# Gated recurrence of a two-block mixer: transposes before state products, the next head's preparation on other levels, masks and values loaded first

## What is computed

```python
def chunk_scan(q, k, v, logf, s0):
    """S_t = diag(f_t) S_{t-1} + k_t v_t^T, o_t = S_t^T q_t, chunkwise. q,k,logf (B,L,H,K); v (B,L,H,V)"""
    def step(S, inp):
        qb, kb, vb, gb = inp
        G = jnp.cumsum(gb, axis=1)
        o_inter = jnp.einsum('bthk,bhkv->bthv', qb * jnp.exp(G), S)
        decay = jnp.exp(jnp.where(earlier_or_same, G[:, :, None] - G[:, None, :], -jnp.inf))
        A = jnp.einsum('bthk,bshk,btshk->bhts', qb, kb, decay)
        o_intra = jnp.einsum('bhts,bshv->bthv', A, vb)
        S_new = jnp.exp(G[:, -1])[..., None] * S + jnp.einsum('bshk,bshv->bhkv', kb * jnp.exp(G[:, -1:] - G), vb)
        return S_new, o_inter + o_intra
```

## Time and profile before

| | us |
|---|---|
| median of three runs | 3906.14 |
| profiled execution | 3909.69 |
| its span | 3907.7 |
| TensorE busy | 3560.9 (91%) |
| VectorE busy | 2585.6 (66%) |
| ScalarE busy | 1877.3 (48%) |
| GpSimd busy | 790.5 (20%) |

### The profile page before, as it was taken

One profiled execution on the slowest core, in us unless ns is written; L12 is line 12 of the kernel. 1 busy time (PEld: TensorE's weight loads), 2 busy tenths in 40 slices (PEclk: granted clock), 3 DMA queues, 4 the chain that ended last, 5 costly groups with the idle time before them and its releaser, 6 DMA issues. The chain is left out here.

```text
span 3907.7 us, 43104 instructions
## 1 busy us (share of the span) xinstructions
PE 3560.9 (91%) x16760; PEld 2846.0 (73%) x16760; DVE 2585.6 (66%) x2881; ACT 1877.3 (48%) x2428; POOL 790.5 (20%) x624
## 2 busy tenths in 40 slices
PE   7999889964697999999999998999898989999989
PEld 4887744664685888888878786788776678787857
DVE  6546266876767888889888887556575545516753
ACT  5211111355463777767777776342464323515731
POOL 2100025500021110111111114210243223203422
PEclk9999989977897999999999999999998999999999
DMA  5554314220236999999999996365411433525133
GB/s 198 201 186 143 124 43 172 84 110 19 94 139 228 379 366 382 378 366 379 376 372 370 362 379 200 107 208 178 168 54 56 164 109 110 165 103 186 48 102 119
DMA packets 322788, 774.50 MB, mean 198 GB/s; under 512 B 26072, under 2 KB 110419, under 8 KB 322328
## 3 DMA queue, kind: packets, MB, share of 16 engines
q1 hardware_dynamic: 299802, 694.94, 48.9%
q0 software_dynamic: 17856, 66.33, 5.2%
q10 hardware_dynamic: 4928, 10.49, 0.8%
HBM read 660.21 MB, written 111.48 MB: 197 GB/s over the span
## 5 line engine op out<-in xcount | busy, mean ns | idle before, releaser
L3398 DVE TENSOR_TENSOR first_expert_w_low<-shared_z,first_expert_w_high 128x2048 fp32r<-128x2048 f32 x127 | 297.1, 2380 | 80.0 <-ACT first_expert_w_high L3351 79.5
L3398 DVE TENSOR_TENSOR moe_w_low<-moe_w_raw,moe_w_high 128x2048 fp32r<-128x2048 f32 x128 | 287.3, 2285 | 52.6 <-ACT moe_w_high L3351 52.1
L3398 DVE TENSOR_TENSOR moe_w_low<-shared_z,moe_w_high 128x2048 fp32r<-128x2048 f32 x128 | 290.5, 2310 | 19.9 <-ACT moe_w_high L3351 19.9
L3351 ACT ACTIVATE first_expert_w_high<-shared_z 128x2048 fp32r<-128x2048 f32 x126 | 234.9, 1918 | 121.0 <-DMA shared_z<-in_exp_w 118.4
L3351 ACT ACTIVATE moe_w_high<-moe_w_raw 128x2048 fp32r<-128x2048 f32 x128 | 238.3, 1911 | 91.2 <-DMA moe_w_raw<-in_exp_w 83.9
L3626 POOL TENSOR_SCALAR layer_att_p<-layer_att_p,layer_att_rinv,layer_att_neg_lam 128x1280 f32<-128x1280 f32 (+1 forms) x72 | 173.4, 2408 | 529.9 <-DVE layer_att_neg_lam L3655 314.2
L3351 ACT ACTIVATE moe_w_high<-shared_z 128x2048 fp32r<-128x2048 f32 x128 | 238.5, 1915 | 54.1 <-DMA shared_z<-in_exp_w 48.3
L177 PE MATMUL moe_bank<-moe_w_high,first_expert_xgT_high 128*128 128x512 f32 x640 | 252.7, 395 | 0.0
L3633 DVE TENSOR_REDUCE layer_att_nb<-layer_att_scores 128x1 f32<-128x1280 f32 (+1 forms) x144 | 195.0, 1369 | 86.4 <-PE layer_att_scores L3538 85.4
L178 PE MATMUL moe_bank<-moe_w_low,first_expert_xgT_high 128*128 128x512 f32 x640 | 250.8, 392 | 0.0
L179 PE MATMUL moe_bank<-moe_w_high,first_expert_xgT_low 128*128 128x512 f32 x640 | 250.6, 391 | 0.0
(11 more groups left out here) (660 smaller groups left out, 9522.1 us busy)
## 6 DMA issues: line engine op xcount, KB each, us to landing
shared_z<-in_exp_w SPq DMA_DIRECT2D x128, 2048.0 KB, 10.1
moe_w_raw<-in_exp_w SPq DMA_DIRECT2D x64, 2048.0 KB, 9.9
shared_z<-in_w_in SPq DMA_DIRECT2D x48, 512.0 KB, 6.2
first_raw<-in_w_in SPq DMA_DIRECT2D x32, 512.0 KB, 7.3
front_vec<-in_ada_w POOLq DMA_DIRECT2D x16, 1024.0 KB, 6.0
proj_t<-front_out SPq DMA_DIRECT2D x48, 256.0 KB, 2.0
shared_z<-in_w_mod SPq DMA_DIRECT2D x24, 512.0 KB, 4.5
k_high<-layer_front_staged SPq DMA_DIRECT2D x20, 512.0 KB
```

The lines of the kernel that those rows point to most:

```text
L3351: nc.scalar.activation(hi, x, ACT.Copy).then_inc(high, 1)
L3398: nc.vector.tensor_tensor(lo, x, hi.bitcast(F32), ALU.subtract).then_inc(low, 1)
```

## The change

Three edits, no instruction added or taken away. SP issues the masks and the values ahead of q and z of head 1. ScalarE does the next head's preparation on other levels: queries at level 1 instead of 5, sigmoids at 2 and 4 instead of 2 and 3, gates at 3 and 5 instead of 3 and 4. TensorE transposes the keys of a level ahead of the state products instead of behind them.

```diff
@@ -2317,10 +2317,10 @@
+                sp.dma_start(mask[:, :, :], io["t_pair_masks"][:, 0:LEVELS * P].rearrange("p (i t) -> p i t", t=P)).then_inc(masks, 16)
+                sp.dma_start(v[:, :, :], core.vg[:, 0:BANK].rearrange("(t p) c -> p t c", p=P)).then_inc(inputs, 16)
                 load_q(1)
                 load_z(1)
-                sp.dma_start(mask[:, :, :], io["t_pair_masks"][:, 0:LEVELS * P].rearrange("p (i t) -> p i t", t=P)).then_inc(masks, 16)
-                sp.dma_start(v[:, :, :], core.vg[:, 0:BANK].rearrange("(t p) c -> p t c", p=P)).then_inc(inputs, 16)
                 for h in range(1, H):
@@ -2427,13 +2427,13 @@
                         if h >= 2 and j in (1, 2):
                             o_copy(2 * (h - 2) + j - 1)
-                        if more and j in (3, 4):
-                            gates(h + 1, j - 3)
-                        if more and j in (2, 3):
+                        if more and j in (3, 5):
+                            gates(h + 1, j // 2 - 1)
+                        if more and j in (2, 4):
                             if (h, j) == (0, 2):
                                 act.wait_ge(zeroed, 1)
-                            sigmoids(h + 1, j - 2)
-                        if more and j == 5:
+                            sigmoids(h + 1, j // 2 - 1)
+                        if more and j == 1:
                             queries(h + 1)
@@ -2531,10 +2531,10 @@
                         for half in range(2):
                             level(h, half, j)
+                        if h and j < NSB:
+                            turn(h - 1, j)
                         if h and 1 <= j <= NSB:
                             state(h - 1, j - 1)
-                        if h and j < NSB:
-                            turn(h - 1, j)
                         for p in (2 * j, 2 * j + 1):
```

## The result

The kernel after took 3871.94 us, the median of four runs (3860.43 to 3874.97), against 3907.84 us for the kernel before in the same session. The ratio is 0.9904, with a 95% interval from 0.9878 to 0.993. In a second session, six runs beside eleven of the kernel before, it was 0.9891 (0.9872 to 0.991). The two ratios make a gain of 37 and 43 us; the medians alone differ by 36 and 41. The forecast was 3867 us, 39 us less than before, with a range of 3856 to 3884.

The account below looks back on a forecast made before the run. VectorE's busy time was taken as each head's floor, with 48.6 us of waiting above it. Gains of 8.0 + 15.4 + 13.3 + 2.6 = 39.3 us gave a 3867 us median, range 3856 to 3884.

Parts of the forecast that it names:

- Part 1: TensorE's transposes put ahead of state products: they no longer stand behind the carry's wait; the delayed state products cost nothing.
- The new chain: Order behind the carry: state products, next level product, next transposes, their copy; head 1's level-3 transposes end at about T+24.1.
- Part 2: ScalarE's preparation spread over levels: 7.1 us in one level become 4.4 at most; gains 15.4 us in head 1, 13.3 in head 2.
- head 1's 3.3 us at level 4: VectorE's remaining stall at level 4, forecast as 3.2 us in head 1 and carried to head 2 as 3.3.
- The 1.2 us at level 2: New VectorE stall in head 2, from output copies ahead of the queries and output products on TensorE; 1.2 us.
- Part 3: Masks and values issued first on SP: the 6.9 us mask stall goes whole, q(1) lands at 818.9, head 0 gains 8.0 us.
- Each us by which q(1) lands later costs one: Head 0: every us of delay in q(1)'s landing was to cost one us.
- the 39.3 of the sum: Total forecast gain of the recurrence stage: 8.0 + 15.4 + 13.3 + 2.6 us for heads 0 to 3.
- A: Rival: more waiting hidden in the heads, by TensorE at full clock; 48 us gone, 3858 us; chance 0.14.
- B: Rival: level 4's stalls in heads 1 and 2 stay 8.9 us behind the carry; gain 28, 3878 us; chance 0.12.
- C: Rival: values ahead of q(1) and z(1) starve ScalarE; slower past 39 us of delay, 3918 us at q(1) 870; chance 0.02.
- D: Rival: waits go but nothing reaches the end, or delayed state products and unseen stalls eat it; 3900 to 3906; 0.05.

Follow-up runs that it names:

- e5_gates_ahead: e4_q_first with ScalarE's first gates at level 3 moved ahead of the copy of the transposes; 3872.09 us in one execution, head 1 45.96 us.
- e1_turn: Kernel before with only TensorE's order changed, transposes ahead of state products; ratio 0.9927, median 3884.21 us.
- e4_q_first: Kernel after with q(1) issued between masks and values; 3858.97 us in one execution, head 0 40.34 us.
- a2_after: The kernel after, unchanged, measured again in the second session against the kernel before; ratio 0.9891.
- e6_fill: Kernel after with 40 unused identity products on TensorE between transposes and state products, head 1, levels 2 and 4; 3876.16 us in one execution.
- e8_fill_short: Kernel after with 20 unused identity products on TensorE between transposes and state products, head 1, levels 2 and 4; 3862.81 us in one execution.
- e10_best: e9_all with the output copies put back at levels 1 and 2; ratio 0.9883 to the kernel before, median 3866.15 us.
- e9_all: Kernel after with q(1) before values, first gates ahead of transposes' copy, output copies at levels 2 and 4, filler products around the tail; ratio 0.9887.

## Why the prediction was right, and where its steps were off

Point by point, in the order of its sum:

- What bounds the kernel: right. VectorE's busy time is the floor, its waits were what went, and head 1 of e5_gates_ahead runs on that floor.
- Part 1: right in mechanism, shown by e1_turn alone: 29.8 us of the heads' 42.5. The 3.4 us that it took for the level product hold for some executions only (2.53 to 3.62 us). The new chain was as I wrote it, and the delayed state products cost nothing: no carry of VectorE waited for them in the heads of the kernel after.
- Part 2, head 1: the stall left at level 4 was put at 3.2 us and measured 2.19, the head at 49.7 and measured 48.29. The mis-sized term was the level product and transposes at half clock, 3.4 and 1.06 us. The clock rose within the group, to 2.86 and 0.60.
- Head 2: 50.9 forecast, 48.09 and 49.56 measured in two executions. I carried head 1's 3.3 us at level 4 over to it. It was 0 in one and 1.77 us in the other, by the clock of the level product. The state products ahead of it ran at full clock (1.13 us) in both, behind 3.2 us of idling where head 1 has 5.6. That the first execution had no stall at all was luck: three of six had one of 1.75 to 1.77. The 1.2 us at level 2 was 1.54, within the 2 us that I had set as the sign of being wrong.
- Head 3: 42.5 forecast, 42.17 measured.
- Part 3: head 0 forecast at 40.6 us, measured 41.99. The masks landed in 3.2 us, where I had 3.3. The values took until 10.9 us after their issue, 8.1 us behind the masks, where I had 6.8, and q(1) came 12.5 us into the stage instead of 11.3. I took 6.8 from a queue that had z(1) ahead of masks and values. What makes the difference no run here shows: in e4_q_first, with masks and q(1) ahead of them, the values took 8.1 us behind q(1) too. The table of the queries was still loaded: no load stands ahead of 823.47. "Each us by which q(1) lands later costs one" fits the 1.2 us late and 1.4 lost, but not beyond: in e4_q_first ScalarE began the queries 5.0 us earlier in the stage and head 0 gained 1.65, with z(1) as the next to be late. Nor did the loss come where I put it, ahead of the last `inner`, but as waits at levels 2 to 4; and my terms add up to 848.0 for the end of the head, not 848.2.
- What I had not counted: 3.15 us given back in the tail by the clock, and a stage start and rest that vary by some us between executions. The heads gained 42.5 us, 3.2 more than the 39.3 of the sum, and the tail took 3.15 of it away: in this execution the stage as a whole, 39.35 us, fits the forecast only because two errors cancel. In a2_after the heads gained 41.4, the tail took 0.3 and the stage gained 41.1. The medians, 3871.94 and 3870.62 us, are 4 to 5 us over the 3867 forecast, less than the spread of start and rest.

Of the rivals, A (more hidden through a faster clock) was half right: granted clocks in heads 1 and 2 rose to 0.82 and 0.85, not the 0.9 that I named for it, and the heads gained 42.5 us and not 48. By the rule cited there from the Trainium skill ("TensorE: Matmul & The Clock Gate", What's actually happening) recent activity releases the clock; e6_fill and e8_fill_short agree, with 1.95 instead of 2.86 us for the product behind a filled gap. B (the stall only changes its name) was refuted as to size: 2.19 us, not 8.9; its loop is real, as e5_gates_ahead showed by taking the rest of it away. C (values ahead of q(1)) is real too, at 1.65 us and far from the 39 at which it would have decided. D is refuted by the ratio.

The trace has no drain behind a table load here either: with the queries at level 1, load and two operations took 3.35 us (861.74 to 865.09). The Trainium skill ("ScalarE: Activation LUTs", What ACT_TABLE_LOAD costs) adds its drain to every switch, which would make it 4.7, an estimate from its 1.38 us; the measurement decides.

## What to carry to other kernels

On an engine whose queue is in order, look at what stands behind a long wait, not only at what waits: an operation with its inputs ready goes ahead of the wait, and then look at what stands behind it now. Other engines' preparation belongs into the time in which they would wait anyway, ahead of their wait and not behind it. A part of 5 us in a program of 3900 is read from the stretch it lies in, since the stretches around it move by as much between executions.

## What was not expected of the hardware

Idle time on TensorE can be paid twice: after 5.6 us of idling the same 24 instructions (state and level products) took 4.5 us to the transposes, and 2.8 us behind a filled gap, 1.14 us of idling ahead of them. But equal idling doesn't mean equal clock: behind 3.20 or 3.21 us of it in head 2 the level product took 1.95 us in three executions and 3.15 to 3.50 in three. And one stretch of equal instructions, the tail, took 26.1 to 26.3 or 23.1 to 23.4 us according to the granted clock, 0.82 or 0.93. Filling a gap is no sure remedy: in e10_best the fill stood behind a slow level product, met half clock itself (4.47 instead of 3.74 us), ended late, and the tail was 2.7 us longer than in e9_all.
